# Hybrid recurrent block on 8 cores: first loads ahead of the parity branch, 8 tokens moved between the parts, late prefix merged with the convolution

## The reference, cut to what matters

```
h = rmsnorm(x, norm_mix_g);  proj = h @ w_in          # 11 slabs of 512 columns
q, f, i, g (512 each) -> HGRN2: S_t = diag(f_t) S_{t-1} + k_t v_t^T, o_t = S_t^T q_t, gated per-head rmsnorm -> @ w_branch_a
c, b, xb (512 each)   -> y = b * causal_conv3(c * xb)                                                      -> @ w_branch_b
merged = sigmoid(gate_a) * y_a + sigmoid(gate_b) * y_b;  x = x + merged @ w_out
x = x + swiglu(rmsnorm(x), w_ffn_gate, w_ffn_up, w_ffn_down)   # 1024 -> 2816 -> 1024
out = rmsnorm(x, norm_final_g)
```

## Time and profile before

| | |
|---|---|
| median of 3 runs | 1015.64 us (1014.77 to 1016.02) |
| the profiled execution's own time | 1016.44 us |
| span of its slowest core, core 4 | 1014.9 us |
| spans of the other even cores 0, 2, 6 | 1011.2, 1010.7, 1011.0 us |
| spans of the odd cores 1, 3, 5, 7 | 1011.2, 1012.0, 1009.9, 1009.5 us |
| core 4: PE, DVE, ACT busy | 974.9, 435.5, 376.3 us |

### The profile page before, as it was taken

One profiled execution on the slowest core, in us unless ns is written; L12 is line 12 of the kernel. 1 busy time (PEld: TensorE's weight loads), 2 busy tenths in 40 slices (PEclk: granted clock), 3 DMA queues, 4 the chain that ended last, 5 costly groups with the idle time before them and its releaser, 6 DMA issues.

```text
span 1014.9 us, 15424 instructions; the slowest of 8 cores (1009.5 to 1014.9 us)
## 1 busy us (share of the span) xinstructions
PE 974.9 (96%) x5574; PEld 526.6 (52%) x5574; DVE 435.5 (43%) x678; ACT 376.3 (37%) x668; POOL 24.6 (2%) x52
## 2 busy tenths in 40 slices
PE   0889999999999999999999999999999999999997
PEld 0435646455556554455555645555464655444455
DVE  3535467776877664566544212122221212223223
ACT  3434285948586742445534111111111111111112
POOL 2000000000000000000000000000000000000000
PEclk9999999999999999999999999999999999999999
DMA  6982405100003544334387040203003053323112
GB/s 125 237 199 46 79 1 94 33 1 2 1 1 55 113 97 112 116 119 140 124 176 150 1 84 1 43 1 64 21 5 79 2 125 125 125 106 119 63 63 59
DMA packets 18947, 78.74 MB, mean 78 GB/s; under 512 B 2224, under 2 KB 2224, under 8 KB 15792
## 3 DMA queue, kind: packets, MB, share of 16 engines
q0 software_dynamic: 6336, 33.03, 18.5%
q1 hardware_dynamic: 12393, 44.38, 13.2%
q10 hardware_dynamic: 135, 0.25, 0.1%
HBM read 93.05 MB, written 17.63 MB: 109 GB/s over the span
## 4 chain that ended last, share of the span: by engine, by line
PE 90%; DMA 4%; ACT 2%; issue 2%; DVE 1%; SPq 1%; POOL 0%; ACTq 0%; DVEq 0%; POOLq 0%
PE pf L830 60%; PE pf L1454 16%; PE pf L841 10%; DMA ring<-wall 3%; DMA ring<-xall 1%; ACT arena L806 1%; PE pf L859 1%; PE pf L1079 1%; SPq L747 0%; ACT L806 0%; PE pf L1254 0%; PE pf L1256 0%; PE pf L1215 0%; PE pf L1234 0%; PE pf L1304 0%
## 5 line engine op out<-in xcount | busy, mean ns | idle before, releaser
L830 PE MATMUL pf<-hT,ring 128*128 128x384 bf16 (+2 forms) x3200 | 607.8, 346 | 6.4 <-DMA ring<-wall 3.2
L830 PEld LDWEIGHTS pf<-hT,ring 128*128 128x128 bf16 x3200 | 311.9, 98 | 273.2 <-issue 11.3
L1454 PE MATMUL pf<-ring,arena 128*128 128x512 bf16 (+2 forms) x735 | 159.8, 373 | 0.0
L806 ACT ACTIVATE rtmp<-pf 128x512 f32<-128x512 f32 (+2 forms) x114 | 59.9, 531 | 203.2 <-PE pf L830 196.5
L1454 PEld LDWEIGHTS pf<-ring,arena 128*128 128x128 bf16 (+1 forms) x735 | 76.2, 105 | 78.1
L810 DVE TENSOR_TENSOR arena<-rtmp,pf 128x512 bf16<-128x512 f32 (+2 forms) x85 | 51.7, 609 | 143.1 <-PE pf L830 129.5
L806 ACT ACTIVATE arena<-pf 128x512 f32<-128x512 f32 (+11 forms) x145 | 77.7, 572 | 75.5 <-PE pf L830 68.8
L830 PE MATMUL pf<-arena,ring 128*128 128x512 bf16 (+2 forms) x320 | 70.8, 345 | 1.5 <-ACT arena L806 1.4
L806 ACT ACTIVATE rtmp<-hT 128x1024 bf16<-128x1024 f32 (+3 forms) x19 | 18.4, 967 | 130.7 <-DVE hT L810 130.7
L841 PE MATMUL pf<-ring,hT 128*128 128x512 bf16 (+1 forms) x272 | 62.6, 379 | 0.0
L806 ACT ACT_TABLE_LOAD x44 | 56.5, 1283 | 6.6 <-DVE sso L1262 3.7
(11 more groups left out here) (101 smaller groups left out, 572.9 us busy)
## 6 DMA issues: line engine op xcount, KB each, us to landing
ring<-wall POOLq DMA_DIRECT2D x24, 1024.0 KB, 11.4
ring<-xall SPq DMA_DIRECT2D x14, 512.0 KB, 8.7
arena<-xall SPq DMA_DIRECT2D x14, 512.0 KB, 4.4
x1spill<-arena SPq DMA_DIRECT2D x14, 512.0 KB, 3.0
hT<-x1spill SPq DMA_DIRECT2D x14, 512.0 KB, 4.4
out<-hT SPq DMA_DIRECT2D x14, 512.0 KB, 2.6
ring<-wall POOLq DMA_DIRECT2D x12, 256.0 KB, 10.6
ring<-wall POOLq DMA_DIRECT2D x6, 512.0 KB, 5.8
```

The costliest lines, as they stand in the source:

```text
L806: P.op("act", lambda E: E.activation(out=rs(out), in_=rs(in_), func=func, **kw), reads=reads, writes=writes, dur=dur, aset=ASET[func] if f ...
L830: last = E.matmul(pb(bk)[:, 0:ncol], lhsT=sl[:, o_:o_ + 128], rhs=rhs[:, c, :], start=(c == 0), stop=(c == kc - 1))
L1454: last = E.matmul(pb(bk)[0:CH, 0:w], lhsT=act_v(c)[:, r0:r0 + CH], rhs=rl[c], start=(c == 0), stop=(c == 21))
```

## The change

- `Prog.mark` notes what SyncE and GpSimd have in their lists up to there: x tiles 0 to 3 and the constants (SyncE), the identity mask and the first two slabs in eight quarters (GpSimd). `emit_both` writes these ahead of the read of the partition number and the branch. As the same instructions must serve both programs, the slabs lie in the weight tensor in the order in which each core loads them (the host prepares two orders).
- The part of the even cores grows by 8 tokens and that of the odd cores shrinks by 8. The even core's last three tiles go from 120 to 124 tokens (2164 in all, 4 of them spare), the odd core's last four from 102 to 100. The prefix grows with the even part.
- In the odd program the last two prefix blocks are merged with the convolution of blocks 1 and 2 instead of standing between them.
- The constants of the gates (`gate_consts`: 2 VectorE and 6 ScalarE instructions) come after the first block's norm.
- `pick` changes: in the even program a bank is given out only if an aligned pair stays free (`strict`); in the odd one single banks go beside held ones first. The oldest waiting TensorE operation is always a candidate.
- The activations of the feed-forward stage are laid out by block, as 22 * 2 * 2164 bytes exceed the area.

```diff
-BL_EVEN = [(4, 128), (4, 128), (3, 128), (3, 128), (3, 120)]
-BL_ODD = [(4, 128), (4, 128), (4, 128), (4, 102)]
+BL_EVEN = [(4, 128), (4, 128), (3, 128), (3, 128), (3, 124)]
+BL_ODD = [(4, 128), (4, 128), (4, 128), (4, 100)]
...
+    def mark(self):
+        self.pre = [o.i for o in self.ops if o.eng in ("sp", "pool")]
+        for i in self.pre:
+            self.ops[i].prio = i - 1e6
...
-                t = max(bank_free[k:k + n])
-                if best is None or t < best[0]:
-                    best = (t, k)
-            return best
+                if strict and not oldest:
+                    rest = [h or k <= j < k + n for j, h in enumerate(held)]
+                    if not any(not rest[j] and not rest[j + 1] for j in range(0, nbanks, 2)):
+                        continue
+                key = (not strict and n == 1 and not held[k ^ 1] and not oldest, max(bank_free[k:k + n]))
+                if best is None or key < best[0]:
+                    best = (key, k)
+            return None if best is None else (best[0][1], best[1])
...
+                if e == "pe" and head_pe < len(pend_pe) and pend_pe[head_pe] in avail[e] and pend_pe[head_pe] not in cand:
+                    cand.append(pend_pe[head_pe])
+                if pre_left[e]:
+                    first = min(i for i in self.pre if ops[i].eng == e and ops[i].fin is None)
+                    cand = [i for i in cand if i == first]
...
     def run(E, e):
+        known = {}
+        odd.run(E, e, known, 0)
         pid = E.partition_id()
         with E.If(pid & 1):
-            odd.run(E, e)
+            odd.run(E, e, dict(known), 1)
         with E.Else():
-            even.run(E, e)
+            even.run(E, e, dict(known), 1)
...
-        UO = O_OG + 16384 if odd else O_MG
+        UO = 16 * max(TOK_EVEN, TOK_ODD)
...
-            idx = names.index(name)
+            idx = nxt["i"] - 1
...
         load_next([None, None, xm[0], xm[1]], 4)
         load_next([xm[1], xm[2], xm[3], xm[3]], 4)
+        P.mark()
...
-            merge((seq(halo_gen(), conv_gen(0, P1S)), 26.0), (npre(3), 2.5))
-            merge((seq(pf_gen(3), pt_gen(2), pv_gen(3)), 16.2), (norm_gen(hTs[1], mn(1)), 2.5))
-            merge((conv_gen(1, P1S), 23.4), (npre(4), 2.5))
-            merge((seq(pf_gen(4), pt_gen(3), pv_gen(4)), 16.2), (norm_gen(hTs[2], mn(2)), 2.5))
-            merge((conv_gen(2, P1S), 23.4), (norm_gen(hTs[3], mn(3)), 2.5), (pt_gen(4), 2.5))
+            merge((seq(halo_gen(), conv_gen(0, P1S)), 26.0), (seq(npre(3), norm_gen(hTs[1], mn(1))), 5.0))
+            merge((conv_gen(1, P1S), 23.4), (seq(pf_gen(3), pt_gen(2), pv_gen(3)), 12.5), (seq(npre(4), norm_gen(hTs[2], mn(2))), 5.0))
+            merge((conv_gen(2, P1S), 23.4), (seq(pf_gen(4), pt_gen(3), pv_gen(4)), 12.5), (norm_gen(hTs[3], mn(3)), 2.5))
+            drain(pt_gen(4))
         else:
             drain(norm_gen(hTs[0], mn(0)))
+            gate_consts()
...
-        P.schedule(8)
+        P.schedule(8, not odd)
```

More of the change, by code:

```diff
@@ L201, in schedule @@
         left = len(ops)
+        pre_left = {e: sum(1 for i in self.pre if ops[i].eng == e) for e in ENGS}
+        pre_set = set(self.pre)
         for o in ops:
@@ L307, in number, with run @@
                     self.val[i] = ("P_" + e, n)
-    def run(self, E, e):
+    def run(self, E, e, known, part):
         ops, val = self.ops, self.val
-        known = {}
         own = "P_" + e
-        for i in self.order[e]:
+        npre = sum(1 for i in self.pre if ops[i].eng == e)
+        for i in self.order[e][:npre] if part == 0 else self.order[e][npre:]:
             o = ops[i]
@@ L330, in run @@
                 o.fn(E).then_inc(self.sems[own], 1)
-        if e == "sp":
+        if e == "sp" and part == 1:
             for b in self.finals:
@@ L341, in emit_both @@
     even.number()
+    assert odd.pre == even.pre
+    for i in odd.pre:
+        assert odd.val[i] == even.val[i] and odd.ops[i].deps == even.ops[i].deps
     def run(E, e):
+        known = {}
+        odd.run(E, e, known, 0)
         pid = E.partition_id()
         with E.If(pid & 1):
-            odd.run(E, e)
+            odd.run(E, e, dict(known), 1)
         with E.Else():
-            even.run(E, e)
+            even.run(E, e, dict(known), 1)
     @block.tensor
@@ L663, in pair, with act_v @@
             return tokpair(i)[0][:, 0:2 * T], pair_b[i, T]
[L665 to L674, removed]
+        act_off = {}
+        at = {"arena": 0, "misc": 0}
+        for j in range(22):
+            for b in range(NB):
+                sp = "arena" if at["arena"] + 2 * TB[b] <= ARENA else "misc"
+                act_off[j, b] = (sp, at[sp])
+                at[sp] += 2 * TB[b]
+        assert at["misc"] <= 6144
+        act_b = [[reg(f"act{j}_{b}", *act_off[j, b], 2 * TB[b]) for b in range(NB)] for j in range(22)]
+        def act_v(j, b):
+            sp, o_ = act_off[j, b]
+            return (arena if sp == "arena" else misc)[:, o_ // 2:o_ // 2 + TB[b]]
         c1s = []
@@ L1591 @@
     SLABS = slab_table()
[L1592 to L1600 removed]
+    walls = {}
+    for odd in (True, False):
+        wall = np.zeros((len(SLABS), 128, 4096), f32)
+        for i, name in enumerate(LOADS[odd]):
+            for kind, key, r0, kc, c0, nc_, off in SLABS[name]:
+                w = W[key][r0:r0 + kc * 128, c0:c0 + nc_].reshape(kc, 128, nc_)
+                if kind == "rhs":
+                    w = w.transpose(1, 0, 2)
+                else:
+                    w = w.reshape(kc, 128, nc_ // 128, 128).transpose(1, 2, 0, 3)
+                wall[i, :, off:off + kc * nc_] = w.reshape(128, kc * nc_)
+        walls[odd] = wall
     in_maps = []
@@ L1609 @@
             xall[0:TOK_EVEN] = x[b, 0:TOK_EVEN]
-        in_maps.append({"xall": xall, "cst": cst, "gf": gf, "wall": wall})
+        in_maps.append({"xall": xall, "cst": cst, "gf": gf, "wall": walls[half == 1]})
     nc = _get_nc()
```

44 lines of the change are left out of this document (20 added, 24 removed).

## The result

The changed kernel took 1037.84 us (median of 4 runs, 1032.83 to 1219.61), the kernel before beside it 1015.2 us. The ratio is 1.0209, 95% interval 1.0162 to 1.0256: slower by some 2%, where 1019.3 was forecast. The profiled execution took 1039.86 us.

The account below looks back on a forecast made before the run. The slowest even core's TensorE matmul chain, with DMA at the start, was taken as the bound: 1014.9 - 9.9 + 3.6 + 5.0 + 5.0 = 1018.6 us span, 1020.1 with overhead, median 1019.3. Range 1008 to 1023.5.

Parts of the forecast that it names:

- Width: Last-block transfers: engines are the largest divisor of the rows up to 16, so 124 rows get 4 and 100 get 10.
- the first rival: 124-row transfers run as wide as those of 120, so both 5 us terms fall away: 1009.3 us, chance 0.18.
- The end: Even cores' last output transfer, on 4 engines, lengthens the program's end by 5.0 us.
- The last `d_gen`: Even cores: tile 16's x read, on 4 engines, lands 7.9 us late; 5 us lost, from 0 to 13.
- The start: Loads ahead of the branch: core 4's program moves 9.9 us earlier, the odd cores start 1.1 us earlier.
- The wait for bg: TensorE's 3.16 us wait on core 4 for slab bg's last quarter stays, as it hangs on the same stream.
- Tokens: Even cores' last block goes from 360 to 372 columns in 716 matmuls: 3.6 us more, all on the path.
- banks: New bank rule in the even program: taken as 0, with up to 5 us either way.
- Third rival: GpSimd's moved branch isn't covered, so the causal mask delays the even cores' first product: 1023 us, chance 0.07.
- Odd cores: Earlier start, fewer columns, shorter end and no `d_gen` wait bring core 3 from 1012.0 to 1002.7 us.

Follow-up runs that it names:

- E3: The kernel before, with every 120-row transfer issued as 116 + 4 rows so that each is narrow, nothing computed differently: 1034.62 us, ratio 1.0216.
- E7: The kernel before, with only the two halves of the even cores' last output tile issued as 116 + 4 rows: 1017.57 us, ratio 1.0042.
- E1: The changed kernel, with every 124-row transfer issued as two, 112 + 12 rows: 1013.26 us, ratio 0.9992.
- E8: The changed kernel, with only the reads of x in the last `d_gen` issued as 112 + 12 rows: 1017.6 us, ratio 1.0039.
- E13: The changed kernel, with only the 124-row spills in `d_gen` issued as 112 + 12 rows: 1018.61 us, ratio 1.0042.
- E14: The changed kernel, with the even cores' five slabs in and just behind the last `d_gen` held until tile 16's x has landed: 1017.31 us, ratio 1.0047.
- E11: The changed kernel with wide transfers as in E1, but nothing loaded ahead of the branch: 1016.71 us, ratio 1.0035.
- E6: E1 with the two programs of the branch exchanged, the even one standing first: 1011.86 us, ratio 0.9983.
- E9: E5 and E6 together: 120 and 102 rows, transfers as 112 + 8 and 96 + 6, even program first: 1007.32 us, ratio 0.9942.
- E4: The changed kernel with all loads behind the branch, as before, and its narrow transfers kept: 1039.08 us, ratio 1.026.
- E2: The changed kernel with the tokens put back, last blocks of 120 rows (even cores) and 102 (odd cores): 1014.54 us, ratio 1.0008.
- E12: E1 with the even cores' bank choice of the kernel before, the earliest free bank: 1015.58 us, ratio 1.0016.
- E5: E2 with its last-block transfers issued as two, 112 + 8 rows on even cores and 96 + 6 on odd ones: 1008.85 us, ratio 0.9955.
- E10: E1 with only x tile 0 left ahead of the branch; constants, other x tiles and both slabs behind it: 1016.45 us, ratio 1.0031.

## Why the prediction was right in direction and wrong in size

**Width: right.** 124 rows ran on 4 engines, 100 on 10; the first rival (as wide as 120) fell with the packet counts and with E3. (The weight slabs, which it named for itself, have 128 rows, a multiple of 16, and could show no narrowing.) What the prediction cited from the Trainium skill, "DMA: Bandwidth & Descriptors", section "Why a DMA increments its semaphore by 16 and not by 1", the trace bears out with 128 and 110 packets.

**The end: right.** Forecast 5.0 us; E7 gives 4.3 (1017.57 less 1013.23).

**The last `d_gen`: this step failed.** It had 5 us, with 13 as the upper end. E1 against E8 isolates the end (with all other narrow transfers but the read; as E7, the end alone, comes out at the same size, they cost nothing); E8 against the changed kernel, this stall. It comes out as 16 to 20 us, by what is compared: 17.2 by the ratios (1.0039 and 1.0209), 20.2 by the medians, 15.7 by the even cores' mean span over all runs. The changed kernel has few runs that scatter widely; E3 less E7, the same stall in the kernel before, is 17.0. I had taken the 10 KB per us of core 3, which makes 24.8 us and a landing at 546.5, and for the bound three slabs. Core 0's timeline shows five. The fourth and fifth are issued at 535.90 and 540.23 us, when TensorE has released the `wo` slots; by my own estimate the read was then still 6 to 11 us from landing. So they run into its last part, and it ended 12 us behind that estimate: 248 KB in 37.6 us, 6.6 KB per us. E13 shows the other side: with less in front the read is there at 537.5, with the fourth slab (issued at 533.04) beside it for its last 4.5 us and the fifth (537.37) not at all, and needs 18.8 us. So any one of the three taken away (the narrow read in E8, the narrow spill in E13, the slabs in E14) brings nearly all of it back. That the late pair of slabs, rather than the first three, sets the difference is argued from their issue times; no run held back these two alone. The read for tile 15 comes late too (VectorE waits 2.1 to 4.1 us on the even cores), but TensorE doesn't stop for it. A second, smaller miss: TensorE lost up to 2 us more at half clock behind the stall, which had no term.

**The start: failed too.** The step "Core 4 gains 12.29 - 2.4 = 9.9 us ... the whole program moves by as much" left out who else has to come through the branch. I moved SyncE's and GpSimd's loads past it and checked their queues, not VectorE's and ScalarE's first instructions, which come by DMA too (q8 and q14, instruction, 10 packets by 30 us on core 0) and now share the engines with the early loads. E11 prices the early loads at 3.4 us (3.8 by the even cores' mean span). The Trainium skill, "Runtime: NRT & Kernel Launch", section "Instruction fetch mechanics", says that a sequencer fetches its instructions by a DMA queue of its own and that a taken branch to a far target must fetch before it goes on; with E11 and E1 this case shows the first instruction behind the taken branch at 6.0 to 6.8 us, against 2.8 in the program that stands first, and at 10.6 to 13.0 with the early loads in flight.

**The wait for bg: wrong.** I left it in, as slab and first product were to move together; no even core has it after. Late norms don't explain that: in E6 and E9 the first product comes at 21.1 to 22.7 us and no even core waits for bg either. Without the early loads (E4, E11) short waits of 0.2 to 0.4 us are back on three of eight cores.

**Tokens, banks.** The columns: 3.6 forecast, 3.9 over all runs (4.6 in the profiled ones), so right. The banks: -2.3 by the medians instead of 0.

**Third rival (the branch not covered): no.** The cast of the mask ends up last on cores 0 and 6, but TensorE's idle time there is 1.86 us, against 1.48 on cores 2 and 4.

**Odd cores.** Forecast 1002.7, measured 1004.8 to 1008.4. The step that failed is the start, "1.1 us earlier": TensorE's wait for slab i was 3.5 to 5.6 us before and is 3.9 to 5.3 after, and the product behind it now starts at 30.9 to 31.9 us instead of 28.5 to 30.2. E2's odd cores are no faster than those of the kernel before, although x starts earlier; what the merged order does behind that point wasn't separated. In the last `d_gen` VectorE still waits 6.4 to 7.3 us for x on three odd cores, with 10 engines, but the 3.6 to 4.4 us of it that reached TensorE before the transposes are gone, as forecast (0.7 to 2.1 us behind ScalarE are left at that place).

The sum. The forecast starts from core 4's 1014.9 us. Measured are the mean spans of the even cores over all runs of a kernel, each less that of the kernel before in its own group (1010.5 us or so, 1011.95 in the one execution beside the changed kernel):

| term | forecast | measured | from |
|---|---|---|---|
| start | -9.9 | -3.8 | E1 less E11 |
| tokens, columns | +3.6 | +3.9 | E1 less E2 |
| bank rule | 0 | -1.6 | E1 less E12 |
| not separated | 0 | +1.0 | what is left to E1, at -0.5 |
| end | +5.0 | +4.4 | E8 less E1 |
| last `d_gen` | +5.0 | +15.7 | changed kernel less E8 |
| sum | +3.7 | +19.7 | changed kernel |

The row "not separated" is what keeps this from being a full account: the place of `gate_consts`, the layout, the oldest operation as a candidate, and how the terms act on each other were in no run of their own. It is about as large as the uncertainty of the rows above it (0.7 to 1 us each); the last row is uncertain by some 3 us, as only three executions stand behind it. Two rows of the forecast were off: the start by 6, the last `d_gen` by 11, and both in the same direction. That the kernel came out slower, as forecast, is no proof of the sum.

## What to carry to other kernels

Before changing the number of rows in a tile, list every transfer of that height and its largest divisor up to 16; for each one that becomes narrow, ask what is queued ahead of it on those few engines and what will be issued beside it before it lands: a transfer that is late can meet the next ones and get later still, which is how I read the 17 us here. Where a height is awkward, issue it as two (112 + 12, 96 + 6): that costs a second issue and gave back 2.2% here, and 0.5% between E2 and E5, where 102 rows had run on 6 engines. When loads are moved ahead of a branch, count all engines' first instructions behind it, and put the program that is slower in the end on the side where the branch costs it less (0.1% here, E6 against E1 and E9 against E5).

## What the runs showed of the hardware

- First instructions behind the branch, in the program that stands second: 6.0 to 7.8 us with nothing in flight (the kernel before, E3, E4, E7, E11), 7.3 to 8.1 with 512 KB (E10), 10.0 to 14.1 with four x tiles and slabs; in the program that stands first 2.8 to 3.0 us with nothing in flight and 3.1 to 4.5 with all of it.
- The program that stands first ended 3.3 to 3.6 us behind SyncE's last wait, the second one 0.6 to 0.9 us, whichever of the two it was (E1, E6), with 5 instruction packets in the last 7 us of the first and none in those of the second.
- The same 248 KB on each of 4 engines (spill and read) took 15.4 us with no slab beside it and 37.6 us with five.
- 124 rows gave 128 packets and 100 rows 110, as 120 had given 135 and 102 had given 108: rows plus the engines that take part. With only narrow transfers of 124 rows moving, the DMA share was 0.24 to 0.25.
